# Sums of a modulation row behind the attention step on TensorE and VectorE, and the last chunk's turned heads ahead of its evictions on ScalarE

## What is computed

```python
sh, sc, gt = jnp.split(jax.nn.silu(c) @ w_ada[l] + b_ada[l], 3, axis=-1)
sh_c, sc_c, gt_c = jnp.split(jax.nn.silu(c_ctx) @ w_ada[l] + b_ada[l], 3, axis=-1)
h = rms_norm(x, norm_g[l]) * (1 + sc[:, None]) + sh[:, None]
hc = rms_norm(ctx, norm_g[l]) * (1 + sc_c) + sh_c
qa, ka, va, ga, qb, kb, vb, gb, qn, kn, vn, gn = split_proj(h @ w_in[l])
...
y = jnp.concatenate([ya, yb, yn], axis=-1) @ w_out[l]     # A: differential, B: grouped, C: neighbourhood attention
ctx = ctx + gt_c * (...)                                  # first layer alone
x = x + gt[:, None] * y
```

## Time and profile before

| | us |
|---|---|
| median of three runs (1193.67 to 1198.55) | 1196.97 |
| the profiled execution | 1194.44 |
| its span | 1192.6 |
| TensorE busy in it | 1114.8 |
| VectorE / ScalarE / GpSimd busy | 724.9 / 600.0 / 262.1 |
| projection `in0` with steps up to 18 ends at about | 263 |
| projection `in1` with steps up to 18 ends at about | 581 |

### The profile page before, as it was taken

How to read it: one execution, slowest core, us unless ns; L and a number is a source line. 1 busy time by engine, 2 the same in 40 slices (tenths; PEclk the granted TensorE clock), 3 DMA queues, 4 the chain that set the end, 5 groups by cost and what they waited for, 6 DMA issues and landing times.

```text
span 1192.6 us, 16740 instructions
## 1 busy us (share of the span) xinstructions
PE 1114.8 (93%) x5877; PEld 892.2 (75%) x5877; DVE 724.9 (61%) x1320; ACT 600.0 (50%) x1176; POOL 262.1 (22%) x324
## 2 busy tenths in 40 slices
PE   5989999998989989999897999999799999999997
PEld 1667677777778777787686887888688887888886
DVE  3487877777764665743456586664655646455543
ACT  3345554444862456645654644453554455544552
POOL 2582521182006151221202031000122202021101
PEclk8999999999999999999999999999899999999999
DMA  8856453425013232232206756556366664444301
GB/s 330 171 177 198 127 157 111 136 88 156 21 56 111 71 119 76 74 92 67 70 2 204 247 155 196 156 176 195 112 206 176 193 182 128 133 124 124 124 1 53
DMA packets 79289, 157.92 MB, mean 132 GB/s; under 512 B 5792, under 2 KB 6088, under 8 KB 78952
## 3 DMA queue, kind: packets, MB, share of 16 engines
q1 hardware_dynamic: 75880, 147.41, 40.0%
q0 software_dynamic: 3328, 9.46, 3.4%
HBM read 153.73 MB, written 3.11 MB: 132 GB/s over the span
## 4 chain that ended last, share of the span: by engine, by line
PE 77%; DVE 10%; ACT 5%; issue 3%; POOL 3%; DMA 2%; SPq 0%; DVEq 0%; POOLq 0%; ACTq 0%
PE bank L773 18%; PE bank L775 18%; PE bank L774 18%; PE bank L922 5%; PE bank L897 4%; PE bank L907 3%; PE bank L999 3%; DVE w_lo L1737 2%; PE bank L972 2%; PE bank L984 2%; POOL small L1539 2%; PE bank L793 2%; DVE work L1757 2%; ACT w_hi L1128 1%; DMA work<-in_w_ada_dram 1%
## 5 line engine op out<-in xcount | busy, mean ns | idle before, releaser
L773 PE MATMUL bank<-w_lo,h_hi 128*128 128x512 f32 (+1 forms) x1152 | 458.0, 398 | 26.7 <-DVE h_lo L1806 10.0
L775 PE MATMUL bank<-w_hi,h_hi 128*128 128x512 f32 (+1 forms) x1152 | 443.6, 385 | 0.0
L774 PE MATMUL bank<-w_hi,h_lo 128*128 128x512 f32 (+1 forms) x1152 | 443.3, 385 | 0.0
L1737 DVE TENSOR_TENSOR w_lo<-raw,w_hi 128x1024 fp32r<-128x1024 f32 x224 | 286.5, 1285 | 169.3 <-ACT w_hi L1128 168.1
L1128 ACT ACTIVATE w_hi<-raw 128x1024 fp32r<-128x1024 f32 x224 | 235.9, 1058 | 268.5 <-PE bank L775 228.2
L773 PEld LDWEIGHTS bank<-w_lo,h_hi 128*128 128x128 f32 x1152 | 219.8, 191 | 76.0 <-issue 27.9
L775 PEld LDWEIGHTS bank<-w_hi,h_hi 128*128 128x128 f32 x1152 | 219.2, 190 | 44.2
L774 PEld LDWEIGHTS bank<-w_hi,h_lo 128*128 128x128 f32 x1152 | 220.1, 191 | 38.5
L922 PE MATMUL bank<-work,stage 128*128 128x128 f32 x640 | 90.3, 281 | 0.0
L1725 POOL TENSOR_TENSOR stage<-stage 128x512 f32<-128x512 f32 x24 | 42.4, 1786 | 217.8 <-DVE stage L551 217.8
L922 PEld LDWEIGHTS bank<-work,stage 128*128 128x128 f32 x640 | 81.6, 197 | 0.9 <-issue 0.4
(11 more groups left out here) (177 smaller groups left out, 1113.9 us busy)
## 6 DMA issues: line engine op xcount, KB each, us to landing
raw<-in_b_w_in_dram SPq DMA_DIRECT2D x80, 512.0 KB, 3.7
raw<-in_w_in_dram SPq DMA_DIRECT2D x56, 512.0 KB, 3.9
raw<-in_a_w_in_dram SPq DMA_DIRECT2D x48, 512.0 KB, 4.3
raw<-in_w_ada_dram SPq DMA_DIRECT2D x32, 512.0 KB, 3.7
work<-in_w_ada_dram SPq DMA_DIRECT2D x16, 512.0 KB, 11.4
raw<-in_w_out_dram SPq DMA_DIRECT2D x16, 512.0 KB, 3.5
raw<-in_a_w_out_dram SPq DMA_DIRECT2D x16, 512.0 KB, 3.5
raw<-in_b_w_out_dram SPq DMA_DIRECT2D x8, 512.0 KB, 3.5
```

The source lines that it names most:

```text
L773: pe.matmul(bank, hT(h_hi, ph, at, tt), w_lo[:, s, k, lo:lo + w], start=first, stop=False)
L774: pe.matmul(bank, hT(h_lo, ph, at, tt), w_hi[:, s, k, lo:lo + w], start=False, stop=False)
L775: mm = pe.matmul(bank, hT(h_hi, ph, at, tt), w_hi[:, s, k, lo:lo + w], start=False, stop=last)
L1737: dve.tensor_tensor(w_lo[:, i % SPLIT, :, :], raw[:, PIECE_AT[p] % RAW, :, :], w_hi[:, i % SPLIT, :, :].bitcast(F32), ALU.subtract).then_i ...
```

## The change

Three things move; no instruction's operands change.

1. On TensorE and on VectorE the sums of a modulation row in `in0` (`ada_total`, `ada_keep`) come behind the attention step of their piece, where they came ahead of it.
2. In the steps themselves (19, 24 and 29) they come behind `turn` and `attend` on TensorE and behind `output` on VectorE, where they came ahead.
3. In chunk 6 of `in0` and of `in1` ScalarE copies chunk 5's last turned heads ahead of tile 0's eviction, where it did so ahead of tile 3's.

```diff
@@ TensorE, project @@
                         else:
                             by_half(ph, c, p, n, after_piece)
+                        if after_piece:
+                            after_piece((p, 1))
                         if p in ADA_READY:
                             ada_total(*ADA_READY[p])
-                        if after_piece:
-                            after_piece((p, 1))
@@ TensorE, attention1.step @@
                     for n in scored_at(units, i):
                         score(units[n], i)
-                    for task in fill.get(i, ()):
-                        if task[0] == "ada":
-                            ada_total(*task[1:])
                     if 0 <= i - 1 < len(units):
                         turn(i - 1)
                     if i >= 2:
                         attend(i - 2)
                     for task in fill.get(i, ()):
+                        if task[0] == "ada":
+                            ada_total(*task[1:])
@@ ScalarE, process_in @@
                 for tt in tiles_of(ph):
-                    if tt == 3:
+                    if tt == (0 if c == PROJ[ph][0] - 1 else 3):
                         turned()
@@ VectorE, attention1.step @@
-                    tasks = fill.get(i, ())
-                    for task in tasks:
+                    if i >= 2:
+                        output(units[i - 2])
+                    for task in fill.get(i, ()):
                         if task[0] == "ada":
                             ada_keep(*task[1:])
-                    if i >= 2:
-                        output(units[i - 2])
-                    for task in tasks:
+                    for task in fill.get(i, ()):
                         if task[0] == "products":
```

## The result

The changed kernel takes **1203.86 us** (median of 4 runs, 1202.77 to 1205.23), the kernel before in the same comparison 1196.3 us (1193.67 to 1198.55). The ratio is 1.0065, with a 95% interval of 1.0047 to 1.0084: 7.6 us slower, where +1.6 was forecast. The profiled execution took 1204.3 us (span 1202.4, against 1192.6 before).

What follows compares the result with a forecast made beforehand. TensorE, busy 93% of the span, was taken as the bound, so only its waits count. Terms 0 + 1.5 - 2.2 - 0.3 + 0 + 2.0 - 0.3 + 0.3 + 0.6 = +1.6 us gave 1198.5, range 1194 to 1204.

Steps and rivals of the forecast that it cites:

- (3, 0): Piece in `in0`: transposes' 1.99 us wait goes, sums wait for two banks; TensorE stands 3.3 us, +1.5, bounds 0 and +3.2.
- the chunk ends: Ends of `in0` and `in1`: ScalarE's moved copy waits, second scores come later; TensorE stands 3.6 and about 3 us.
- turn 17: TensorE transposes at both chunk ends: 0.4 of 1.10 us saved in `in0`; idle time before it in `in1` down to 0.6.
- (4, 0): Piece in `in0`: 0.50 us wait covered and low-clock stretch of 1.7 gone, -2.2 us, bounds -2.2 and 0.
- my terms for waits: The forecast's place-by-place us for TensorE's changed waits, leaving out the prices put on half-clock stretches.
- steps 24 and 29: Later sums: step 24 -0.3 us (bounds -1.4 and 0), step 29 +0.3 us (bounds -0.6 and +0.5).
- (5, 0): Piece in `in0`: 1.74 us wait for `ada_keep` replaced by some 1.4 for `keep_turned`, -0.3 us, bounds -2.6 and +1.
- I price that at most of one stretch, +1.5: End of `in0`, with step 19: extra cost of the low-clock stretch lying behind a longer idle time and over longer work.
- the end of `in0`: With step 19: +0.5 at full clock plus +1.5 for low clock, +2.0 us, bounds +0.5 and +4.
- half clock behind the longer waits: Rival: idle times of 3 us or more each bring a 1.7 us stretch, four in all; +8.4, 1205 us; chance 0.13.
- the end of `in1`: Second scores go from 586.64 to 587.2 behind ScalarE's wait, +0.6 us, bounds +0.5 and +2.3.
- the prediction's own sign: Wrong if second scores at the chunk ends don't come later, or if the time leaves 1191 to 1203.

## Why the prediction was wrong

**Right: the places and the waits.** The idle times came out as worked out, 3.2 for 3.3 at (3, 0), 3.53 for 3.6 and 2.76 for about 3 at the chunk ends, 0.66 for 0.6 before turn 17, the copy's 2.52 for 2.45. (4, 0) brought -2.1 for -2.2. Taken without the clock, my terms for waits add to +1.5 - 0.5 - 0.3 + 0.5 + 0.6 = +1.8; steps 24 and 29 cancel. Measured are +2.6 in both pairs of traces. The order of the work on each engine, ScalarE's above all, accounts for most of that; 0.8 us more was idle than my terms give.

**(5, 0).** Forecast -0.3. By waits alone it is near: the sum waits 1.27 us for `keep_turned` (forecast 1.4), in place of 1.74:

```profile
207.28 3.17 PE L698 MATMUL bank<-ones,work 128*128 128x1 f32 x16 [1.27 <-ACT stage L1329]
```

But the one-column sums now lie in the low stretch, which costs 3.4 us there against 1.7, and that is most of what turned -0.3 into +1.7. In the second trace of the changed kernel this place took 18.78, +0.1.

**The step that failed: "I price that at most of one stretch, +1.5".** The clock's terms in my sum were -1.7 at (4, 0) and +1.5 at the end of `in0`, near zero together, with nothing at (3, 0), (5, 0) and `in1`. In the first trace they came to -1.7, then +3.4, +1.7, +5.1 and +1.7, and +7.2 of busy time over the whole. At three places the measured move lies outside the bounds that I gave: (3, 0) with +4.2 over +3.2, (5, 0) with +1.7 over +1, the end of `in0` with +5.1 over +4. The rival "half clock behind the longer waits" had this mechanism, with 1205 for its time, and I gave it 0.13. That its time came so near is in part luck: it counted one more stretch at (3, 0), one in `in1`, one more in `in0`, and kept the one after (4, 0), where the trace has two, one and three, another at (5, 0), and none after (4, 0). My evidence against it was that 2.04 us and 1.99 us of idle time had brought no stretch. That was one draw each. Later traces with the very order of before show what another draw gives: (3, 0) took 21.58 with the third edit alone, which does not touch it, and the end of `in1` 36.38 with the second edit alone, behind the same 2.04 us of idle time.

**The cause, as far as it is shown.** Useless matmuls in the idle time bring the changed kernel from 1.0065 back to 1.0031 or 1.0012 (chunk ends alone, 64 or 128 rows) or to 0.9989 (everywhere); nothing but TensorE's clock and its idle time is touched by them. So of the 7.6 us, 2.6 are waits, read from two pairs of traces, and the 5 that are left are half clock. The granted clocks of all runs say the same, +4.6 of low clock and +2.6 of the rest. Where a stretch begins, and why one order of instructions has it in one execution and not in another, stays open. The third edit carries most: 1.0038 alone. The first is worth +1.3 us and can't be told from nothing; the second is -1.9. The parts add to +3.9 by their ratios, the whole is +7.8; the intervals (each about 2 us to either side) leave open whether the edits make each other worse, and no run settled it.

The Trainium skill says of this in "TensorE: Matmul & The Clock Gate", under "A second HAM failure mode: psum-queue depth-cycling", that in one kernel short idle times between groups of matmuls came often enough to make the clock swing, and that the loss lies in the throughput between bursts. The traces agree: in one of them the low clock behind 0.96 us of idle time cost the same 6.8 us as behind 3.53. The section "What's actually happening" of that page calls the count of slow matmuls at the start of a kernel "run-variable". Here the same holds in the middle of one: 20.00 and 21.58 us at (3, 0) for one order of instructions.

**The range.** 1194 to 1204 held the median by 0.1 us, which is luck; by the prediction's own sign, a time outside 1191 to 1203, it was wrong. With 0.86 on no change the chances were too sure. The time lost to the clock alone differs by 6.8 us (22.2 and 29.0) between two traces of one kernel; a forecast that rests on one of them should have said so.

## What to carry to other kernels

When an edit lengthens an idle time of TensorE, price the wait from the order of the queues, and beside it the half-clock stretch that may follow, as a chance and not as a yes or no read from one trace. A copy that is moved ahead of evictions on a queue that does not pass must find its data ready: ahead of tile 0 it cost 4.5 us, ahead of tile 1 nothing that could be measured. Where the wait can't be removed, useless matmuls in the idle time can be worth more than they cost: eleven of them took the changed kernel from 1.0065 to 0.9989 of the one before.

## What the runs showed of the hardware that was not expected

- Sixteen records of one-column matmuls take 1.84 to 1.92 us at full clock, as long as four records of 512 columns (1.88), and 3.41 to 3.57 where the clock is low. So the busy time of the profile does not tell how many columns TensorE works through.
- The clock fell behind 0.96 us of idle time and 3.70 us of matmuls on 64 rows. In another kernel with the same instructions there it stayed full behind 0.95 us and the same 3.70 us, and so it did behind 0.94 us and matmuls on 128 rows (2.76 us). One trace each; the cause is open.
- The time lost to the low clock came at nearly every place as 1.7 us or a multiple of it: 1.7, 3.4, 5.1, 6.8.
